# Who makes the low half of the expert down weights, and who empties the down product's two PSUM banks

## What is computed

```
for e in range(N_EXPERTS):
    a = jax.nn.silu(t @ w_exp_gate[e]) * (t @ w_exp_up[e])
    y = y + combine[:, e:e + 1] * (a @ w_exp_down[e])
```

## Time and profile before

| | us |
|---|---|
| median of 3 runs (1327.07 to 1328.45) | 1328.09 |
| the profiled execution: device time | 1326.43 |
| its span in the profile | 1324.6 |
| expert stage, from the first gather's issue to the last down product's end | 905.6 to 1282.6 |
| 14 tiles in the steady part (966.18 to 1236.56, from one issue of a `Wd` load to another) | 270.38, or 19.31 a tile |

### The profile page before, as it was taken

How to read it: one execution, slowest core, us unless ns; L and a number is a source line. 1 busy time by engine, 2 the same in 40 slices (tenths; PEclk the granted TensorE clock), 3 DMA queues, 4 the chain that set the end, 5 groups by cost and what they waited for, 6 DMA issues and landing times.

```text
span 1324.6 us, 19929 instructions
## 1 busy us (share of the span) xinstructions
PE 1147.9 (87%) x7062; PEld 1030.9 (78%) x7062; DVE 882.3 (67%) x1276; ACT 661.9 (50%) x994; POOL 366.4 (28%) x161
## 2 busy tenths in 40 slices
PE   5899999999999999799999989553999999999930
PEld 3498988999889899699999989343787777777720
DVE  4456696977869777665665372673777877778617
ACT  2345657566575665522222111450676677667514
POOL 0032222222212222133333322222054334324221
PEclk9899999999999999799999999775999999999975
DMA  9624512212122122043334450633599999999655
GB/s 371 156 88 140 154 42 72 67 62 74 52 73 64 60 76 68 19 169 132 127 130 158 165 183 32 252 145 111 214 350 387 399 363 384 395 364 368 243 168 216
DMA packets 64706, 234.92 MB, mean 177 GB/s; under 512 B 17776, under 2 KB 32512, under 8 KB 56448
## 3 DMA queue, kind: packets, MB, share of 16 engines
q1 hardware_dynamic: 60608, 219.32, 45.7%
q0 software_dynamic: 4032, 14.68, 3.0%
HBM read 209.85 MB, written 24.13 MB: 177 GB/s over the span
## 4 chain that ended last, share of the span: by engine, by line
PE 22%; DMA 17%; DVE 10%; issue 4%; ACT 4%; POOL 1%; DVEq 0%; SPq 0%; POOLq 0%; ACTq 0%
PE PS L679 17%; DMA Wg<-in_experts 14%; PE PS L869 3%; DVE WgLo L1732 3%; ACT WgHi L1149 3%; DVE acc L1475 1%; DMA slot_rows<-Ys 1%; DMA hS<-h_rows,idxc 1%; PE PS L777 1%; POOL WdLo L582 1%; PE PS L824 1%; DVE sq L1570 1%; DMA adaL<-in_w_ada_late 1%; DVE rank L1582 1%; DVE xo L1790 0%
## 5 line engine op out<-in xcount | busy, mean ns | idle before, releaser
L567 POOL TENSOR_TENSOR wLo<-wRaw,wHi 128x1024 fp32r<-128x1024 f32 x80 | 205.2, 2566 | 580.4 <-ACT wHi L948 580.4
L679 PE MATMUL PS<-hHi,wHi 128*128 128x320 f32 x896 | 289.0, 323 | 10.7 <-issue 5.5
L679 PE MATMUL PS<-hLo,wHi 128*128 128x320 f32 x896 | 280.6, 313 | 0.0
L679 PE MATMUL PS<-hHi,wLo 128*128 128x320 f32 x896 | 280.5, 313 | 0.0
L679 PEld LDWEIGHTS PS<-hHi,wHi 128*128 128x128 f32 x896 | 172.3, 192 | 14.0 <-issue 9.1
L679 PEld LDWEIGHTS PS<-hLo,wHi 128*128 128x128 f32 x896 | 172.2, 192 | 0.0
L679 PEld LDWEIGHTS PS<-hHi,wLo 128*128 128x128 f32 x896 | 171.7, 192 | 0.0
L582 POOL TENSOR_TENSOR WdLo<-Wd,WdHi 128x2048 fp32r<-128x2048 f32 x18 | 86.4, 4800 | 227.2 <-ACT WdHi L1149 227.2
L948 ACT ACTIVATE wHi<-wRaw 128x1024 fp32r<-128x1024 f32 x80 | 84.2, 1052 | 87.5 <-PE PS L679 67.4
L1475 DVE SCALAR_TENSOR_TENSOR acc<-adaL,csil,acc 128x512 f32<-128x512 f32 x112 | 104.7, 993 | 12.9 <-DMA adaL<-in_w_ada_late 12.4
L1732 DVE TENSOR_TENSOR WgLo<-Wg,WgHi 128x2048 fp32r<-128x2048 f32 x34 | 77.1, 2310 | 49.5 <-ACT WgHi L1149 49.5
(11 more groups left out here) (319 smaller groups left out, 2815.7 us busy)
## 6 DMA issues: line engine op xcount, KB each, us to landing
wRaw<-in_wtiles SPq DMA_DIRECT2D x80, 512.0 KB, 3.4
Wg<-in_experts SPq DMA_DIRECT2D x18, 2048.0 KB, 12.3
Wu<-in_experts SPq DMA_DIRECT2D x18, 2048.0 KB, 11.3
Wd<-in_experts SPq DMA_DIRECT2D x18, 2048.0 KB, 10.4
adaL<-in_w_ada_late SPq DMA_DIRECT2D x32, 512.0 KB, 4.1
slot_rows<-Ys SPq DMA_DIRECT2D x18, 512.0 KB, 11.3
ada<-in_w_ada SPq DMA_DIRECT2D x8, 1024.0 KB, 18.2
slot_rows<-tab SPq DMA_DIRECT2D x10, 512.0 KB, 6.4
```

The costliest lines, as they stand in the source:

```text
L567: nc.gpsimd.tensor_tensor(wLo[b][:], wRaw[b][:], wHi[b][:].bitcast(F32), ALU.subtract).then_inc(w_lo, 1)
L679: r = mm(PS[:, bank, 0:HALF], w[:, k, :], x[:, k, cols], start=(k == 0 and w is wHi[b] and x is xh), stop=(k == KT - 1 and w is wLo[b]))
```

## The change

GpSimd no longer works on the weights: `down_low` and its semaphore `Wd_loP` go, and VectorE makes both halves of the down weights' low part. In exchange VectorE no longer copies its half of the down product; ScalarE takes both PSUM banks in one instruction of 128x1024. One semaphore `ys_ev` takes the place of two.

```
         def load(x, t, ex):
             wait(sp, W_lo_ok[x], t)
-            if x == 2:
-                wait(sp, Wd_loP, t)
...
         def rows_out(t, b):
-            sp.wait_ge(ys_evA, t + 1)
-            sp.wait_ge(ys_evD, t + 1)
+            sp.wait_ge(ys_ev, t + 1)
...
-        def down_low(t):
-            pool.wait_ge(W_hi_ok[2], 2 * t + 2)
-            pool.sem_inc(ticks, 1)
-            weights_low(2, slice(KT // 2, KT)).then_inc(Wd_loP, 1)
-        down_low(0)
...
             for b in range(2):
-                down_low(2 * j + 1 + b)
                 gather(2 * j + 4 + b, b)
         seq.leave(more + (E // 2 - 2))
-        for t in range(E - 3, E):
-            down_low(2 * more + t)
...
         def down(t):
             pe.wait_ge(at_lo, t + 1)
             pe.wait_ge(W_lo_ok[2], t + 1)
-            pe.wait_ge(Wd_loP, t + 1)
-            wait(pe, ys_evA, t)
-            wait(pe, ys_evD, t)
+            wait(pe, ys_ev, t)
...
-                A(Ys[1 - b][:, 0:512], PS[:, 6, :], ACT.Copy).then_inc(ys_evA, 1)
+                A(Ys[1 - b][:].rearrange("p (h c) -> p h c", h=2), PS[:, 6:8, :], ACT.Copy).then_inc(ys_ev, 1)
...
         def weights_low(x, t):
-            for k in range(0, KT if x < 2 else KT // 2, 4):
+            for k in range(0, KT, 4):
                 dve.wait_ge(W_hi_ok[x], 2 * t + (k // 4 + 1))
...
-            if before:
-                dve.wait_ge(d_mm, t)
-                wait(dve, ys_out[1 - b], ro)
-                v.tensor_copy(Ys[1 - b][:, 512:1024], PS[:, 7, :]).then_inc(ys_evD, 1)
-                if not rows_only:
-                    weights_low(2, t)
+            if before and not rows_only:
+                weights_low(2, t)
```

More of the change, by code:

```diff
@@ L307, in build @@
     W_in, W_hi_ok, W_lo_ok = ([sem(f"W{n}_{x}") for n in "gud"] for x in ("in", "hi_ok", "lo_ok"))
-    Wd_loP = sem("Wd_loP")
     ht_mm, ht_hi, ht_lo, at_hi = sem("ht_mm"), sem("ht_hi"), sem("ht_lo"), sem("at_hi")
@@ L311, in build @@
     W_mm = [g_mm, u_mm, d_mm]
-    th_ok, a_ok, at_lo, ys_evA, ys_evD = sem("th_ok"), sem("a_ok"), sem("at_lo"), sem("ys_evA"), sem("ys_evD")
+    th_ok, a_ok, at_lo, ys_ev = sem("th_ok"), sem("a_ok"), sem("at_lo"), sem("ys_ev")
     ys_out = [sem(f"ys_out{i}") for i in range(2)]
@@ L1739, in h_low, with expert @@
                             hSH[b][:].bitcast(F32), ALU.subtract).then_inc(ht_lo, 1)
-        def expert(t, b, ro, last=False, rows_only=False):
+        def expert(t, b, last=False, rows_only=False):
             before = not (isinstance(t, int) and t == 0)
@@ L1770, in _ @@
         h_low(0, 0)
-        expert(0, 0, 0)
-        expert(1, 1, 0)
-        expert(2, 0, 0)
+        expert(0, 0)
+        expert(1, 1)
+        expert(2, 0)
         with nc.vector.Fori(0, more + (E // 2 - 2)) as j:
             seq.enter(j, 2)
-            expert(2 * j + 3, 1, 16 * (j + 1))
-            expert(2 * j + 4, 0, 16 * (j + 1))
+            expert(2 * j + 3, 1)
+            expert(2 * j + 4, 0)
         seq.leave(more + (E // 2 - 2))
-        expert(2 * more + (E - 1), 1, 16 * more + 8 * (E - 2), last=True)
-        expert(2 * more + E, 0, 16 * more + 8 * (E - 2), last=True, rows_only=True)
+        expert(2 * more + (E - 1), 1, last=True)
+        expert(2 * more + E, 0, last=True, rows_only=True)
         dve.wait_ge(gb_in, 48)
```

## The result

The changed kernel takes 1292.86 us (median of 4 runs, 1286.05 to 1295.09), the kernel before 1327.58 beside it. The ratio is 0.9741, 95% interval 0.9707 to 0.9775: 2.6% less time, where 1.3% was forecast. The profiled execution took 1291.51 us.

A forecast was written before the change was run, and what follows sets the result against it. Bound: a loop of loads, ScalarE and VectorE, with transfers nearly full and TensorE close behind. 8.1 + 0.7 + 4.8 + 3.7 - 0.3 = 17.0 us off 1326.43, plus 1.66 for the median: 1311 us, range 1301 to 1321.

The forecast's parts named there:

- the steady part: 14 tiles of the expert loop: the `Wd` load issued 2.2 us earlier closes the idle DMA time, 8.1 us less.
- the three signs: Against the prediction: share rises while GB/s fall; `WgLo` starts late behind `aTL`; chain runs through TensorE in the expert loop.
- Rival 2: Expert loop: rounds come down to TensorE's pace, 17.94 us a tile, 19.2 us less, 1300 us in all; chance 0.08.
- The first tiles: Way into the expert loop: GpSimd's and VectorE's subtractions no longer slow each other, 0.7 us less.
- The first gather: Start of the expert stage: second `Wd` load leaves later, so the gather's wait falls from 10.83 us; 4.8 us less.
- The end: End of the expert stage: last two `WdLo` give 2.2 and 1.5 us, 3.7 less; longer last copy, 0.3 more.
- The gather's place: GpSimd's gather in the expert loop: starts at nearly the same point of a round, same bytes; costed at nothing.
- The copy and VectorE's longer list: Expert loop: ScalarE's larger copy, 0.43 us more, and VectorE's extra 2.29 us subtraction are covered by waits; costed at nothing.
- Rival 1: Expert loop stays as it is, an earlier load only waits longer in its queue; 8.9 us less, 1319.2; chance 0.22.
- rival 3: Expert loop slower: a queue without holes puts every gather beside a load; 9.3 us more, 1337.4; chance 0.06.
- Rival 4: Start of the expert stage: the first gather gains nothing, the rest as forecast; 12.2 us less, 1315.9; chance 0.06.

The follow-up runs named there:

- the two half changes: Changed kernel with VectorE keeping its copy of the down product's upper half: 1290.11 us; kernel before with only that copy moved to ScalarE: 1325.6 us.

## Why the prediction was right and where it was wrong

The direction was right, and so was the mechanism of the steady part as far as the load that goes out 2.3 us earlier; what that is worth was not. 1311 was forecast, 18.1 us too much. Two of the three signs that the prediction named as being against it came true: `WgLo` starts directly behind `aTL`, and the chain runs through TensorE.

- **The steady part, 8.1 us: mis-sized.** The step that failed reads "the idle DMA time in a tile is 0.03 x 19.31 = 0.58 us on average [...] so I take it that it closes". It measured 22.2 us, 14.1 more. The load did go out 2.3 us earlier, as forecast. But the share counts a transfer system as busy whose load has only begun and moves at 260 GB/s, and I had the reason at hand: "says nothing on how fast a fuller queue runs". The rate of the microseconds in which the queue is filled, about 430 GB/s in both traces, would have given 7.34 MB / 430 = 17.1 us a tile, below TensorE's own time. Rival 2, TensorE's pace, came true at 17.73 (it said 17.94, from a window of one round; 19.2 us for the steady part against 22.2), and it had got a chance of 0.08.
- **The first tiles, 0.7 us**: 3.2 measured. 2.3 of it is that the load at which I cut goes out earlier in its round, which the forecast had booked at the end; 0.9 stay for the term.
- **The first gather, 4.8 us**: 5.2 measured, and shown by the pair of runs with the first half back on GpSimd, 10.98 against 5.68 us.
- **The sorting, not in the sum**: 5.0 us. I had seen VectorE and GpSimd slow each other, and priced it only on the way into the loop. GpSimd's first `WdLo` lies in the sorting, where VectorE is on the chain. `ohT` accounts for 4.05 of it; another 0.6 is `rank`, which meets GpSimd's `WuLo` in both kernels, for 7.19 us before and 6.57 after; it varies from 6.2 to 7.2 in the traces, so this part is scatter.
- **The end, 3.7 - 0.3 us**: 3.7 measured, which is luck, since it is made up otherwise than from 2.2 and 1.5: 1.0 from the last round and its load, 1.7 from the start of the last `WdHi` to the down product (7.1 us, before 8.8), and 1.0 because that product itself took 7.45 us instead of 8.41. The last copy takes 1.03.
- **The gather's place, costed at nothing**: the step "it starts at nearly the same point of a round" failed. The gather goes out 5.3 to 7.7 us behind the `Wd` load, and before it was 0.7 in all rounds but the first. Held back to 1 us behind the load, it costs 0.14 us a tile, so the error was small.
- **The copy and VectorE's longer list, costed at nothing**: right, by the two half changes. The cover of `WgLo` did vanish in some rounds, but VectorE isn't what ends last.
- **Scatter**: the profiled execution of the changed kernel lost 4.2 us ahead of the experts, against it. Over the terms, 14.1 + 2.5 + 0.4 + 5.0 + 0.3 - 4.2 is 18.1, or 17.9 before rounding (34.9 of the spans less 17.0); the medians give 18.1.

Rival 1 (an earlier issue only waits longer) and rival 3 (a fuller queue is slower) are refuted: the rate rose. Rival 4 fell with the first gather.

What stays open: how the cost of a late load splits between its start on idle engines and the second stretch, and what makes the second stretch slow. That lateness costs time by itself is shown by one pair, 0.51 us a tile for 1.2 us of delay. By all the runs, the pace is 17.73, 18.24, 18.87 and 20.32 at delays of 6.67, 7.87, 8.95 and 10.9 us, but the gather's place isn't the same in all of them. By single profiles it is worth 0.14 us a tile at the first delay, 0.54 at 7.8 and 0.44 at 8.95; the whole times bear out neither of the last two.

## What to carry to other kernels

A DMA share near 1 is no proof of a full transfer system. Read the GB/s beside it in windows of a microsecond around each issue, and compare it with the best rate in the same trace: that, times the bytes of a round, is what the round could come down to, and the next engine's busy time is the floor. Where a single buffer is refilled, the delay from "landed" to "issued again" is what to shorten. Before giving work to GpSimd, look for VectorE instructions beside it that have grown to its length, above all outside the loop that you mean to change.

## What the runs showed of the hardware

- A VectorE instruction whose tensors all lie in SBUF and that meets a running GpSimd subtraction waits for its end, however short it is; in the traces of these kernels none ended before it: 4.35 us for 0.30 (128x26), 3.42 for 1.23 (128x1024), 8.46 for 0.82 (`sq`). Those that read PSUM, such as `aTL`, ran at 0.68 us beside it. "GPSIMD Engine Reference", section 1. Specifications, of the Trainium skill says that the two share SBUF interfaces, with contention when VectorE has two SBUF inputs or a 2-port mode; the rows agree for the two-input instructions (the mode of `ohT` isn't in the trace) and add that the loss can be nearly the whole of GpSimd's instruction.
- GpSimd's writing of the gather's descriptors takes 0.96 us, and longer when it begins while a VectorE subtraction runs. Over all 18 traces there are 133 such cases, and 132 of them took 2.2 to 4.8 us (all but one 3.0 or less); the last, near the end of a subtraction of 1.23 us, took 1.22. In 94 more a subtraction begins only within the writing, and those took 0.96 to 0.99. Who starts first decides.
- A load that starts on idle DMA engines moves at about 260 GB/s in its second microsecond, with a DMA share of 0.95 on average: in the window shown, its packets of 16 KB take 1.15 us instead of 0.61.
